# A wait for its own matmuls, behind the first round of each up projection, on TensorE

## The chip, the core and the metric

The kernel runs on one core of one Trainium2 chip. What counts is the time of one execution on the device, in microseconds (us). TensorE (PE in the profile) does the matrix products and loads their weights (PEld), VectorE is DVE, ScalarE is ACT, GpSimd is POOL, and SyncE (SP) issues nearly all of the loads.

## What is computed

Two transformer blocks on 256 tokens of width 2048, in float32. Each block has a mixer (the first two kinds of attention, the second a gated linear recurrence) and behind it a gated feed-forward part of width 5632. The change lies in the feed-forward parts alone:

```
# first block
u = causal_dwconv(h @ w_up[l], conv_w[l], conv_b[l])
gate, up = jnp.split(u, 2, axis=-1)
y = (jax.nn.gelu(gate, approximate=True) * up) @ w_down[l]
x = x + rms_norm(y, post_ffn_norm[l])
...
# second block
up = dwconv3(h @ w_in, w_conv)
gate, val = jnp.split(up, 2, axis=-1)
return (jax.nn.silu(gate) * val) @ w_out
```

`h @ w_up[l]` and `h @ w_in` are the up projections: 256 tokens by 2048 by 11264. The kernel calls them "up1" and "up2", and the projections behind them "down1" and "down2".

## The kernel before

Every product keeps float32 precision by splitting both operands into a high and a low part and summing three products of them: high by high, high by low and low by high. The kernel is one stream of weight chunks. A chunk is 256 rows of a weight matrix by 512 columns (512 KB), and chunks go through a ring of four buffers (`RING`). SyncE loads chunk n into `raw`, ScalarE writes its high part `whi` (L214, `split_hi`), VectorE its low part `wlo` (L219, `split_lo`), and TensorE uses both. Three semaphores count chunks over the whole program: `hi_done`, `lo_done` and `chunk_used`. The last one is raised by the last matmul of a chunk when that matmul has ended, so that its value is the number of chunks that TensorE is through with.

An up projection (`up_pe`) has 11 rounds. A round is 16 chunks (`BODY`): eight for 512 columns of the gate half, gathered in the banks `acc`, and eight for 512 columns of the up half, in the banks `tp`. A chunk is worked by `products_turned`: for each of two slices of 128 rows and each of four tiles of 128 columns, the high weights are loaded and the high and low activations stream past in one matmul of 512 columns (L252), then the low weights are loaded and the high activations stream past in one of 256 columns (L254). One L252 with the L254 behind it is called a pair in this document; a chunk has 8 pairs, a round has 128.

Round 0 is written out (`body(0, True)`), because the turning of the activations (transposes, L306 and L318, and the copies into `ahl` on ScalarE and VectorE, L326 and L337) is woven into its first half, and between its halves stands one small product for the row scale (L574, recorded as two matmuls). Rounds 1 to 10 are a loop of the hardware (`pe.Fori`, L577), whose code stands once. Behind them comes the down projection (`back_pe`, L232 to L234), in three matmuls of 512 columns per step. The order on TensorE is the order of the code; no scheduler moves anything. TensorE's sequencer works through instructions, register steps and waits in this order and hands the matmuls to the engine, ahead of it.

Of the kernel before, what the change touches and what calls it, by code (L numbers as in the profile page):

```python
# [55 lines left out]
def bass_two_blocks(nc, T):  # L56
    with ExitStack() as ctx:
# [5 lines left out]
        def sem(name):  # L63
            if name not in made:
                made[name] = ctx.enter_context(nc.semaphore(name))
            return made[name]
# [120 lines left out]
        hi_done, lo_done, chunk_used = sem("hi_done"), sem("lo_done"), sem("chunk_used")  # L187
# [3 lines left out]
        cb, gb = {}, {}  # L191
# [49 lines left out]
        def products_turned(pe, n, s, half, k0, ready=None, row=None):  # L241

            pe.wait_ge(lo_done, n + 1)
            for k in range(CK):
                kt = k0 + k
                if ready:
                    pe.wait_ge(sem("pre_lo"), lo_ready(ready, kt))
                for ct in range(4):
                    c, o = slice(k * GC + ct * P, k * GC + (ct + 1) * P), part_banks(half, ct // 2)
                    if row and k == 0 and ct == 3:  # L250
                        pe.wait_ge(row, NT + 2)
                    pe.matmul(o[:, ct % 2, :].rearrange("p (a t) -> p a t", a=2), whi[:, s, c], ahl[:, :, kt, :],  # L252
                              start=(kt == 0), stop=False, skip_group_check=True)
                    mm = pe.matmul(o[:, ct % 2, 0:S], wlo[:, s, c], ahi[:, kt, :], start=False, stop=(kt == KT - 1),  # L254
                                   skip_group_check=True)
            mm.then_inc(chunk_used, 1)

        def group(pe, g):

            if not (isinstance(g, int) and g < 2):  # L260
                pe.wait_ge(group_free, g - 1)
# [79 lines left out]
        def lead_pe(pe, ph, c, src, ready):  # L341

            if c == 0:
                pre_pe_by_token(pe, ph, src, ready)
            for q in {2: (2,), 4: (3,)}.get(c, ()):
                pre_pe(pe, ph, q, src, ready)
# [204 lines left out]
        BODY = 2 * CPG  # L551
# [8 lines left out]
        def up_pe(pe, ph, src_ready):  # L560
            def body(i, first):
                for c in range(BODY):
                    if c % CPG == 0 and not first:
                        group(pe, gb[ph] + c // CPG + i * 2)
                    if first:
                        lead_pe(pe, ph, c, x, src_ready)
                    if first and c == 0:
                        pe.wait_ge(group_free, gb[ph])
                    products_turned(pe, cb[ph] + c + i * BODY, c % RING, c // CPG, CK * (c % CPG),
                                    ph if first and c < CPG else None, sem(f"{ph}_row") if first and c == CPG else None)  # L570
                    if first and c == CPG - 1:
                        pe.wait_ge(sem(f"{ph}_row"), NT)
                        pe.wait_ge(sem("ones"), 2)
                        pe.matmul(tp[1][:, 2, :], upones[:, :], cvu[:, 0, :], start=True, stop=True)\  # L574
                          .then_inc(sem(f"{ph}_row"), 1)
            body(0, True)
            with pe.Fori(1, FG) as i:  # L577
                body(i, False)

# [1472 lines left out]
        @block.tensor  # L2052
        def _(pe):
            setup_pe(pe)
            m1_pe(pe)
            up_pe(pe, "up1", x_ready("out1"))
            back_pe(pe, "down1", 1, DCH, sem("up1_hid"))
            m2_pe(pe)
            up_pe(pe, "up2", x_ready("out2"))
            back_pe(pe, "down2", 3, DCH, sem("up2_hid"))  # L2060
# [73 lines left out]
```

## Time and profile before

| what | us |
|---|---|
| median of three timed runs | 2535.77 |
| the three runs | 2527.97, 2535.77, 2537.52 |
| the profiled execution, its own time | 2534.18 |
| its span, first to last instruction | 2532.2 |
| up1: rounds 1 to 10, first matmul of round 1 to first of down1 | 500.35 to 952.62 |
| up2: the same | 1841.21 to 2284.95 |

The trace is of one execution. The three timed ones differ from each other by up to 9.55 us, which is 0.38% of the time. TensorE's busy share is 99% of the span, and its granted clock is 0.999, so that it stands at the higher of its two levels, 2.4 GHz. Ends of matmuls in the profile are modelled; starts are recorded, and a pace is therefore best read from one start to another.

### The profile page before, as it was taken

Reading aid. Unit: us, or ns where it says so; the run is one execution under the profiler, and the core shown is the slowest. Engines: PE = TensorE matmul, PEld = TensorE weight load, DVE = VectorE, ACT = ScalarE, POOL = GpSimd, SP = SyncE. Lnnn points to the kernel's source line nnn. Section 1 sums busy time; section 2 is a strip of 40 time slices with the busy share of each in tenths; the row PEclk is TensorE's granted clock in tenths of the full one; section 3 lists DMA queues with packets and bytes.
Section 4 is the critical chain, followed back from the end, with each engine's and each line's share of the span. In section 5 each row is a group of like instructions: output and inputs, shape, how many; then the busy total and the mean of one; then the engine's idle time right before and its main releaser. Section 6 shows DMA issues by size and latency. Waiting matters only on the chain.

```text
span 2532.2 us, 40555 instructions
## 1 busy us (share of the span) xinstructions
PE 2514.1 (99%) x15445; PEld 2159.4 (85%) x15445; DVE 1651.8 (65%) x2018; ACT 1334.9 (53%) x1753; POOL 222.1 (9%) x94
## 2 busy tenths in 40 slices
PE   9999999999999999999999999999999999999998
PEld 9999877888888888888888888888888888888887
DVE  6665574777676775445586868785667677775444
ACT  5454563655556554444545455454665656554443
POOL 1000000022131221000000000000012121121000
PEclk9999999999999999999999999999999999999999
DMA  7765335566666656556655555555566666666554
GB/s 232 252 205 155 113 127 182 169 183 182 190 186 187 183 182 215 192 191 193 191 176 167 175 153 171 162 163 178 173 189 187 190 189 188 185 194 212 192 193 156
DMA packets 241432, 462.26 MB, mean 183 GB/s; under 512 B 14360, under 2 KB 23377, under 8 KB 240673
## 3 DMA queue, kind: packets, MB, share of 16 engines
q1 hardware_dynamic: 239633, 453.44, 58.0%
q0 software_dynamic: 1568, 7.10, 0.9%
q8 instruction: 86, 1.41, 0.2%
q14 instruction: 33, 0.27, 0.0%
q10 hardware_dynamic: 112, 0.03, 0.0%
HBM read 458.40 MB, written 2.12 MB: 182 GB/s over the span
## 4 chain that ended last, share of the span: by engine, by line
PE 99%; DVE 0%; ACT 0%; issue 0%; POOL 0%; DVEq 0%; POOLq 0%; ACTq 0%
PE acc L232 13%; PE acc L252 13%; PE tp L252 13%; PE acc L234 13%; PE acc L233 13%; PE tp L254 7%; PE acc L254 7%; PE acc L918 3%; PE acc L920 2%; PE acc L921 2%; PE acc L1145 1%; PE acc L1147 1%; PE acc L1146 1%; PE tp L1627 1%; PE acc L926 1%; PE acc L928 1%
## 5 line engine op out<-in xcount | busy, mean ns | idle before, releaser
L219 DVE TENSOR_TENSOR wlo<-raw,whi 128x1024 fp32r<-128x1024 f32 x856 | 1070.7, 1258 | 748.1 <-ACT whi L214 746.5
L214 ACT ACTIVATE whi<-raw 128x1024 fp32r<-128x1024 f32 x856 | 903.1, 1059 | 1005.1 <-PE acc L234 456.2
L252 PE MATMUL acc<-ahl,whi 128*128 128x512 f32 x1408 | 494.2, 395 | 0.6 <-DVE ahl L337 0.6
L252 PE MATMUL tp<-ahl,whi 128*128 128x512 f32 x1408 | 494.2, 395 | 0.0
L254 PE MATMUL tp<-ahl,wlo 128*128 128x256 f32 x1408 | 394.8, 280 | 0.0
L254 PE MATMUL acc<-ahl,wlo 128*128 128x256 f32 x1408 | 394.6, 280 | 0.0
L252 PEld LDWEIGHTS acc<-ahl,whi 128*128 128x128 f32 x1408 | 264.0, 187 | 62.6 <-issue 1.0
L252 PEld LDWEIGHTS tp<-ahl,whi 128*128 128x128 f32 x1408 | 263.9, 187 | 61.9
L232 PE MATMUL acc<-whi,ahl 128*128 128x512 f32 x752 | 298.8, 397 | 0.3 <-DVE ahl L337 0.3
L234 PE MATMUL acc<-whi,ahl 128*128 128x512 f32 x752 | 293.4, 390 | 0.0
L233 PE MATMUL acc<-wlo,ahl 128*128 128x512 f32 x752 | 292.8, 389 | 0.0
L254 PEld LDWEIGHTS tp<-ahl,wlo 128*128 128x128 f32 x1408 | 266.0, 189 | 0.1
L254 PEld LDWEIGHTS acc<-ahl,wlo 128*128 128x128 f32 x1408 | 266.0, 189 | 0.0
L233 PE MATMUL acc<-wlo,hhi 128*128 128x512 f32 x672 | 261.4, 389 | 0.0
L234 PE MATMUL acc<-whi,hlo 128*128 128x512 f32 x672 | 261.4, 389 | 0.0
L232 PE MATMUL acc<-whi,hhi 128*128 128x512 f32 x672 | 261.4, 389 | 0.0
L718 POOL TENSOR_TENSOR cvg<-cvg,cvu 128x1024 f32<-128x1024 f32 x22 | 98.1, 4457 | 1499.4 <-DVE cvu L662 1499.4
L234 PEld LDWEIGHTS acc<-whi,ahl 128*128 128x128 f32 x752 | 141.1, 188 | 30.2
L232 PEld LDWEIGHTS acc<-whi,ahl 128*128 128x128 f32 x752 | 141.2, 188 | 29.6 <-issue 0.5
L233 PEld LDWEIGHTS acc<-wlo,ahl 128*128 128x128 f32 x752 | 141.3, 188 | 27.8
L918 PE MATMUL acc<-ahl,whi 128*128 128x256 f32 x512 | 150.5, 294 | 0.0
L233 PEld LDWEIGHTS acc<-wlo,hhi 128*128 128x128 f32 x672 | 126.1, 188 | 26.3
(271 smaller groups left out, 2968.2 us busy)
## 6 DMA issues: line engine op xcount, KB each, us to landing
raw<-in_w_up_dram SPq DMA_DIRECT2D x176, 512.0 KB, 3.8
raw<-in_ffn_w_in_dram SPq DMA_DIRECT2D x176, 512.0 KB, 4.1
raw<-in_hgrn_w_in_dram SPq DMA_DIRECT2D x160, 512.0 KB, 3.7
raw<-in_w_in_dram SPq DMA_DIRECT2D x88, 512.0 KB, 3.8
raw<-in_w_down_dram SPq DMA_DIRECT2D x88, 512.0 KB, 3.7
raw<-in_ffn_w_out_dram SPq DMA_DIRECT2D x88, 512.0 KB, 3.7
raw<-in_w_out_dram SPq DMA_DIRECT2D x32, 512.0 KB, 3.6
raw<-in_hgrn_w_out_dram SPq DMA_DIRECT2D x32, 512.0 KB, 3.9
```

The source lines that it names most:

```text
L214: act.activation(whi[:, s, :], raw[:, s, :], ACT.Copy).then_inc(hi_done, 1)
L219: dve.tensor_tensor(wlo[:, s, :], raw[:, s, :], whi[:, s, :].bitcast(F32), ALU.subtract).then_inc(lo_done, 1)
L232: pe.matmul(out[:, t, :], xh, whi[:, s, c], start=(kt == 0), stop=False)
L233: pe.matmul(out[:, t, :], xh, wlo[:, s, c], start=False, stop=False)
L234: mm = pe.matmul(out[:, t, :], xl, whi[:, s, c], start=False, stop=(kt == nk - 1))
L252: pe.matmul(o[:, ct % 2, :].rearrange("p (a t) -> p a t", a=2), whi[:, s, c], ahl[:, :, kt, :], start=(kt == 0), stop=False, skip_group_ch ...
L254: mm = pe.matmul(o[:, ct % 2, 0:S], wlo[:, s, c], ahi[:, kt, :], start=False, stop=(kt == KT - 1), skip_group_check=True)
L718: pool.tensor_tensor(cvg[:, :, :], cvg[:, :, :], cvu[:, :, :], ALU.mult).then_inc(sem(f"{ph}_pr"), 1)
L918: pe.matmul(o[:, d], whi[:, s, a], ahi[:, kt, :], start=first and ct % 2 == 0, stop=False, skip_group_check=True)
L920: pe.matmul(o[:, d], whi[:, s, a], alo[:, kt, :], start=False, stop=False, skip_group_check=True)
L921: mm = pe.matmul(o[:, d], wlo[:, s, a], ahi[:, kt, :], start=False, stop=last, skip_group_check=True)
L926: pe.matmul(out[:, t, :], xh, whi[:, s, a], start=first, stop=False)
```

## The change

One wait is added in `up_pe`, between the code of round 0 and the loop over rounds 1 to 10. It runs once in up1 and once in up2.

```
             body(0, True)
+            pe.wait_ge(chunk_used, cb[ph] + BODY)
             with pe.Fori(1, FG) as i:
                 body(i, False)
```

`cb[ph]` is the number of chunks before this projection, and `BODY` is 16, so that TensorE waits for the end of the last matmul of round 0. No instruction is moved; from here on, the lines behind it bear a number higher by one.

TensorE's instructions around the end of round 0 of up1, before the change. `tp` is the bank of the up half, `acc` that of the gate half; the rows of L577 and the row of L243 are steps of the sequencer.

```order
L252 MATMUL tp1<-ahl,whi 128x512
L254 MATMUL tp1<-ahl,wlo 128x256
L577 UNCONDITIONAL_BRANCH
L577 ISA
L243 ISA [waits group_free]
L252 MATMUL acc0<-ahl,whi 128x512 [waits lo_done]
L254 MATMUL acc0<-ahl,wlo 128x256
```

The same place with the change:

```order
L252 MATMUL tp1<-ahl,whi 128x512
L254 MATMUL tp1<-ahl,wlo 128x256
L578 UNCONDITIONAL_BRANCH [waits chunk_used]
L578 ISA
L243 ISA [waits group_free]
L252 MATMUL acc0<-ahl,whi 128x512 [waits lo_done]
L254 MATMUL acc0<-ahl,wlo 128x256
```

The wait stands ahead of the loop's entry, so that the entry's register steps and all the loop's matmuls are behind it. In up2 the same rows stand, with the same wait, and nothing else on any engine differs.

## Rows read from the trace of the kernel before

**Rows 1.** The page's head, its busy shares and its clock slices, TensorE alone.

```profile
span 2532.2 us, 40555 instructions
...
PE 2514.1 (99%) x15445; PEld 2159.4 (85%) x15445; DVE 1651.8 (65%) x2018; ACT 1334.9 (53%) x1753; POOL 222.1 (9%) x94
...
PEclk9999999999999999999999999999999999999999
```

**Rows 2.** The page's chain that ended last, by engine.

```profile
PE 99%; DVE 0%; ACT 0%; issue 0%; POOL 0%; DVEq 0%; POOLq 0%; ACTq 0%
```

**Rows 3.** Waits of TensorE: waiter, waited for, us in total, times, longest.

```profile
PE acc L1145 <- DVE ahl L1460: 2.8, 1, 2.8
...
PE acc L252 <- DVE ahl L337: 0.6, 2, 0.3
```

**Rows 4.** Windows, matmuls of L252 alone: each stretch, its us, then busy (count).

```profile
core 0: us, PE busy (x) PEld busy (x), PEclk, DMA share, GB/s
453.50:458.35 4.85, 4.85 (x15) 2.62 (x15) 1.00 0.35 100
459.93:464.78 4.85, 4.85 (x15) 2.62 (x15) 1.00 0.72 209
466.36:476.95 10.59, 10.59 (x31) 5.62 (x31) 1.00 0.45 143
478.09:500.35 22.26, 22.26 (x65) 11.84 (x64) 1.00 0.71 217
500.35:952.62 452.27, 452.27 (x1281) 240.40 (x1280) 1.00 0.62 185
1794.99:1799.84 4.85, 4.85 (x15) 2.62 (x15) 1.00 0.35 102
1801.42:1806.27 4.85, 4.85 (x15) 2.62 (x15) 1.00 0.72 208
1807.84:1818.23 10.39, 10.39 (x31) 5.62 (x31) 1.00 0.46 147
1819.37:1841.21 21.84, 21.84 (x64) 11.78 (x64) 1.00 0.70 213
1841.21:2284.95 443.74, 443.74 (x1281) 239.25 (x1280) 1.00 0.63 189
```

**Rows 5.** Timeline of TensorE around the start of round 1 in up1: start, us.

```profile
500.23 0.28 PE L254 MATMUL tp<-ahl,wlo 128*128 128x256 f32 x1
500.35 0.40 PE L252 MATMUL acc<-ahl,whi 128*128 128x512 f32 x1
```

**Rows 6.** The line L337, VectorE: ns of one, first and last start.

```profile
L337 DVE SCALAR_TENSOR_TENSOR ahl<-tp,gains,ahl x4: 476/479/484, 452.4 to 453.6; 128x256 fp32r<-128x256 f32 x4
```

**Rows 7.** Timeline where TensorE restarts behind that line, up1's first matmuls.

```profile
452.45 1.66 DVE L337 SCALAR_TENSOR_TENSOR ahl<-tp,gains,ahl 128x256 fp32r<-128x256 f32 x4 [0.36 <-ACT ahl L326]
453.05 0.19 PEld L252 LDWEIGHTS acc<-ahl,whi 128*128 128x128 f32 x1 [0.49 <-issue]
453.08 0.47 PE L252 MATMUL acc<-ahl,whi 128*128 128x512 f32 x1 [0.28 <-DVE ahl L337]
...
453.38 0.28 PE L254 MATMUL acc<-ahl,wlo 128*128 128x256 f32 x1
...
453.73 0.28 PE L254 MATMUL acc<-ahl,wlo 128*128 128x256 f32 x1
```

**Rows 8.** Lines L577 and L243 on TensorE's sequencer: ns min/median/max, first and last start.

```profile
L577 PEldq FUSED_REGOPS  x20: 50/50/50, 497.3 to 2237.8; - x20
...
L577 PEldq COMPARE_BRANCH  x20: 76/208/236, 542.5 to 2281.9; - x20
L577 PEldq MOVE  x2: 33/34/34, 497.2 to 1838.1; - x2
...
L243 PEldq FUSED_REGOPS  x20: 37/37/42, 497.4 to 2237.9; - x20
```

**Rows 9.** Waits of all engines in rounds 1 to 10 of up1.

```profile
DVE wlo L219 <- ACT whi L214: 134.9, 110, 2.1
ACT whi L214 <- PE acc L254: 112.9, 70, 1.8
```

More of the change, by code:

```diff
@@ L576, in up_pe @@
             body(0, True)
+            pe.wait_ge(chunk_used, cb[ph] + BODY)
             with pe.Fori(1, FG) as i:
```

## The prediction

> **What bounds the kernel now.** I read the page first: TensorE is busy for 99% of the span at a granted clock of nine tenths or more in every slice [rows 1], and the chain that ended last is TensorE for 99% [rows 2]. Its waits are few: the longest is 2.8 us, and in the up projections there is one wait for `ahl` at the start of each, 0.6 us for the two [rows 3]. So in the up projections the time is the number of matmuls by the distance from one start to the next, and nothing else. Here the windows show what decides this case [rows 4]. Rounds 1 to 10 have 1280 pairs in either projection, the same code at the same granted clock, 1.00. In up1 they take 452.27 us, which is 353.3 ns a pair, and in up2 443.74 us, 346.7 ns a pair. At 2.4 GHz these are 848 and 832 cycles, 16 apart. The DMA share is 0.62 and 0.63, so the load traffic doesn't tell them apart. I call them the slow and the quick pace; the slow one costs 8.53 us over the ten rounds. VectorE and ScalarE follow at either: they wait for one another and for TensorE [rows 9], and TensorE for none of them.
>
> **Where a pace is taken and where it is kept.** Up to its loop each projection has four places at which a new run of pairs starts: once behind a wait with the engine empty (453.08), twice right behind transposes, once behind the product of the row scale. From the windows between [rows 4], by start-to-start steps: up1 has 4.85/14 = 346 ns, 4.85/14 = 346 ns, then 10.59/30 = 353 ns, 22.26/63 = 353 ns, and the loop at 353.3. Up2 has 346, 346, 10.39/30 = 346, 21.84/63 = 347, and the loop at 346.7. So the slow pace came in at one start, the third of up1 (behind transposes that followed on matmuls without a wait), outlived the row product, and was then held for all of 1280 pairs; in up2 it never came. The pace is a state of the stream, taken when the stream starts and kept while it isn't broken. Both starts behind a real wait, in up1 and in up2, were quick; they run for only 14 steps, which is enough to see the pace. The loop's entry in before is no break: its register steps start at 497.2 to 497.4 [rows 8], while the matmul behind them starts at 500.35 [rows 5], so the sequencer is some 3 us ahead and the stream goes through.
>
> **The wait itself.** What it costs is worked out for up1. The last matmul of round 0 starts at 500.23 and lasts 0.28, so it ends at 500.51, while the next one started at 500.35 [rows 5]: 0.16 us of overlap is lost. From the end of what is waited for to the first matmul I take TensorE's restart at 453.08: `ahl` ended at 452.45 + 0.48 = 452.93 [rows 6, 7], so 0.15 us. The loop's entry steps, hidden before, now stand behind the wait: MOVE, FUSED_REGOPS of L577 and that of L243, from 497.2 to some 497.44 [rows 8], about 0.25 us. The first L254 comes 0.30 us behind its L252 in a restart (453.08 to 453.38), where the usual distance in the quick pace is 0.35 less 0.12, that is 0.23 [rows 5, 7]: 0.08 us. Sum 0.64 us, twice 1.28 us. The wait's lower bound is without the entry steps, 0.39 us. Its upper bound adds the dearest branch, 0.24 us [rows 8], for code that must be fetched: 0.88 us. So 0.8 to 1.8 us for both; I take 1.3, since the entry steps follow the wait in the program.
>
> Nothing else pays. Queued behind the wait on TensorE are only the loop's own matmuls; for them wait ScalarE's next `whi` (L214) and with it VectorE and the loads, which have had to wait for TensorE anyway, 112.9 us of it at `acc` alone in up1 [rows 9]. For those 0.6 us they go on filling the ring. SP's and POOL's queues aren't moved. The clock has no reason to fall: the break is about as long as the wait at the projection's start (0.3 us), where the window behind it shows 1.00 [rows 3, 4].
>
> **A rule set against the rows.** The rows have a pair at 346.7 or 353.3 ns [rows 4]. The Trainium skill, page "TensorE: Matmul & The Clock Gate", section "Back-to-back issue gap", gives start to start as the columns over 2.4 GHz plus 2.5 ns for an isolated matmul, which would be an estimated 325 ns a pair, whatever happened before. It knows no second pace; neither row agrees with it. The same page, section "Step-by-step: what each phase is for", says that the drain of one matmul overlaps the fill of the next, and that this is what makes a stream quick. That speaks against the change: by it, breaking the stream can only lose, and the first rival below would be the outcome.
>
> **The forecast.** The wait empties the engine, so each loop's pace is taken anew at a start of the kind that was quick both times. Up1's loop then goes from 452.27 to 443.74 us, up2's stays at 443.74. From the profiled execution's own time: 2534.18 - 8.53 + 1.28 = 2526.9 us. The median before, 2535.77, lies 1.6 above that execution. Of the three timed runs one took 2527.97, and the others 7.8 and 9.55 more: about the 8.53 of one loop. I read this as an execution with both loops quick and two with one slow loop, so that the kernel before draws its pace in every run. With the change the median would come down to where that quick run was. I give 2527.0.
>
> **The rivals.** First, the wait only costs: the pace depends on something that the wait doesn't reset, or one of the two loops still falls into the slow one in the typical run. For it: slow came at one of only eight starts, so two quick starts behind waits are what chance would mostly give as well. Against it: in this trace the pace was seen to change at a start and nowhere else. Time: 2534.18 + 1.28 = 2535.5 us, no change. Second, on the other side: the start behind the wait lands on the slow pace in both loops. Unlike the starts at 453.08, it comes right behind the engine's own last matmul, with a fixed delay of about half a microsecond, and a fixed delay could fix the bad phase as well as the good one. The price is 8.53 us in up2's loop, 1.28 for the waits, nothing gained in up1: 2534.18 + 9.81 = 2544.0 us. It decides if the restart is 16 cycles a pair slower in more than one loop. Against it are again the two quick starts. Third, the sequencer's lead of 3 us is lost and not won back, and then each turn of the loop shows its branch, 0.24 us and some register steps [rows 8]: 18 turns by about 0.4 us is 7 us on top of the forecast, 2534 us. Against it: after the restart at 453.08 the lead must be built too, and by 497.2 it is 3 us. Fourth, the wait does nothing since the matmuls have ended when it is reached; the sequencer's lead rules that out [rows 5, 8].
>
> **How the numbers follow.** Both loops quick in the typical run: 0.54, at 2525.5 to 2529 (bounds of the wait, and the quick timed run at 2527.97). One loop slow or the wait only costing: 0.30, at 2534 to 2538. Both slow: 0.09, at 2542 to 2546. Lead lost: 0.03. Something unseen, such as a third pace, in either direction: 0.04. The range 2524.5 to 2538.5 takes in the first two and the fourth, 0.87 of the chance; it can't be narrower, as the two likeliest cases lie one loop apart. What a measurement can tell from no change is 0.5%, here 12.7 us, more than one loop's pace is worth. All four cases lie within it (2527.0 is 0.35% below the median, 2544.0 is 0.32% above), so: faster by over 0.5% 0.04, within 0.5% 0.93, slower by over 0.5% 0.03.
>
> **What the profile after would show.** A restart gap in front of the first L252 of round 1 in both projections, 0.5 to 0.9 us from the L252 before it would have come. Rounds 1 to 10: 443.7 us each if I am right; one or both at 452.3 for the rivals. Entry steps of L578 right ahead of that matmul rather than 3 us ahead. In turns of the loop no distance between pairs above 0.36 us; if they show 0.6, the lead is lost. I am wrong in the mechanism if a pace changes in mid-loop, or if both loops are slow behind waits in every run.

## The result, and the profile after

The kernel before has a median of 2532.15 us over 22 runs, the changed one 2537.08 us over 22; the ratio is 1.0029, with a 95% interval of 1.0016 to 1.0043. The change makes the kernel slower, by about 0.3% (the two medians differ by 0.19%, the two means by 0.25%): less than the 0.5% that the prediction took as its bound, but not in the direction that it forecast.

The times don't scatter around a middle. They fall into three groups some 9 us apart, with nothing between them. The median of before even lies in a gap: it is the mean of 2528.53 and 2535.77, and no run took anything near it.

| | up to 2531 | 2533 to 2539 | over 2542 | slow loops |
|---|---|---|---|---|
| before, 22 runs | 11 | 8 | 3 | 14 of 44 |
| changed, 22 runs | 3 | 9 | 10 | 29 of 44 |
| before, all 160 runs of this study | 73 | 74 | 13 | 100 of 320 |

8.53 us is what rounds 1 to 10 of one up projection cost more at the slow pace than at the quick one ([rows 4] of before). So I read a group as the number of loops that ran slow: none, one, two. The last column counts them so. The profiled executions bear it out: those of 2534.18 us (before) and 2535.38 us (changed) have one slow loop, one of 2543.6 us (below) has two, and one of 2527.76 us has none. Over all 160 runs the groups of before have the means 2526.9, 2535.7 and 2545.0 us. They are a little more than 8.53 us apart; in the trace of before the slow pace held from the third start of round 0 on, which is 93 steps more, 0.6 us. The change moved the share of slow loops from 14 of 44 to 29 of 44 (were each loop drawn by itself with one chance, a difference of this size would come up about once in 400 such comparisons), and that, not the wait's own time, is most of the loss.

The profiled execution of the changed kernel took 2535.38 us (span 2533.3). Its chain is TensorE, as in [rows 2], and the clock is the same:

```profile
span 2533.3 us, 40555 instructions
...
PE 2514.7 (99%) x15445; PEld 2159.5 (85%) x15445; DVE 1651.9 (65%) x2018; ACT 1335.0 (53%) x1753; POOL 222.2 (9%) x94
...
PEclk9999999999999999999999999999999999999999
```

The windows of L252 in the changed kernel, to be held against [rows 4]; each row has the stretch, its us, and busy (count). The first two stretches are 14 steps from pair to pair at the very start of up1 and of up2, the third and the last but one are 30 steps ahead of the row product, the fourth and the last are the loops:

```profile
453.31:458.16 4.85, 4.85 (x15) 2.61 (x15) 1.00 0.34 103
1786.93:1791.88 4.95, 4.95 (x15) 2.64 (x15) 1.00 0.35 105
...
466.17:476.77 10.60, 10.60 (x31) 5.63 (x31) 1.00 0.46 144
500.66:944.51 443.85, 443.84 (x1280) 239.36 (x1280) 1.00 0.63 188
1799.88:1810.27 10.39, 10.39 (x31) 5.62 (x31) 1.00 0.46 144
1833.76:2286.12 452.36, 452.36 (x1280) 240.51 (x1280) 1.00 0.62 185
```

Up1 came to the wait in the slow pace (10.60/30 = 353 ns) and left it in the quick one (443.85 us for the loop); up2 came quick (10.39/30 = 346 ns) and left slow (452.36 us). In this execution the wait exchanged the two loops of before and cost its own time. The second row matters as well: behind the wait for `ahl` at the start of up2, with the engine empty, the pace is 4.95/14 = 354 ns, the slow one. In the trace of before both starts of this kind were quick. Over the eleven traces in which this start is unchanged (before, the changed kernel, and nine of the kernels below), 9 of 22 such starts were slow.

The wait itself, TensorE's timeline in up1 (start, us), against [rows 5]:

```profile
499.70 0.28 PE L254 MATMUL tp<-ahl,wlo 128*128 128x256 f32 x1
499.81 0.40 PE L252 MATMUL tp<-ahl,whi 128*128 128x512 f32 x1
500.04 0.28 PE L254 MATMUL tp<-ahl,wlo 128*128 128x256 f32 x1
500.67 0.49 PE L252 MATMUL acc<-ahl,whi 128*128 128x512 f32 x1 [0.34 <-DVE wlo L219]
501.00 0.28 PE L254 MATMUL acc<-ahl,wlo 128*128 128x256 f32 x1
501.12 0.40 PE L252 MATMUL acc<-ahl,whi 128*128 128x512 f32 x1
```

The step from L252 to L252 across the wait is 0.86 us where 0.35 is usual, the next is 0.45, together 0.61 us more. The releaser that is named is `wlo`; the wait that the edit puts there is the one for TensorE's own matmul, and I read the gap as that one. The steps of the loop's entry now stand right ahead of the matmul at 500.67, where in [rows 8] they were 3 us ahead of it:

```profile
L578 PEldq FUSED_REGOPS  x20: 50/50/50, 500.5 to 2238.1; - x20
...
L578 PEldq MOVE  x2: 29/32/34, 500.4 to 1833.5; - x2
```

### The profile page after: what moved, and what is told of

It reads as the page before. It is cut to its first block, busy times and chain, and to the rows that moved or that the text cites. A ratio compares the mean times of both kernels' runs of the same rounds, so it can differ in the third digit from the quotient of the medians.

```text
span 2533.3 us, 40555 instructions
## 1 busy us (share of the span) xinstructions
PE 2514.7 (99%) x15445; PEld 2159.5 (85%) x15445; DVE 1651.9 (65%) x2018; ACT 1335.0 (53%) x1753; POOL 222.2 (9%) x94
## 4 chain that ended last, share of the span: by engine, by line
PE 98%; ACT 1%; DVE 0%; issue 0%; POOL 0%; DVEq 0%; ACTq 0%; POOLq 0%
PE acc L232 13%; PE acc L252 13%; PE acc L234 13%; PE acc L233 13%; PE tp L252 13%; PE acc L254 7%; PE tp L254 6%; PE acc L919 3%; PE acc L922 2%; PE acc L921 2%; PE acc L1146 1%; PE acc L1148 1%; PE acc L1147 1%; PE tp L1628 1%; PE acc L927 1%; PE acc L929 1%
## 5 line engine op out<-in xcount | busy, mean ns | idle before, releaser
L219 DVE TENSOR_TENSOR wlo<-raw,whi 128x1024 fp32r<-128x1024 f32 x856 | 1070.6, 1258 | 749.4 <-ACT whi L214 747.7
L252 PE MATMUL acc<-ahl,whi 128*128 128x512 f32 x1408 | 494.5, 395 | 1.3 <-DVE wlo L219 0.7
L252 PE MATMUL tp<-ahl,whi 128*128 128x512 f32 x1408 | 494.2, 395 | 0.0
L252 PEld LDWEIGHTS acc<-ahl,whi 128*128 128x128 f32 x1408 | 264.0, 187 | 63.9 <-DVE wlo L219 1.3
L252 PEld LDWEIGHTS tp<-ahl,whi 128*128 128x128 f32 x1408 | 263.9, 187 | 61.9
```

The lines of the kernel that those rows point to most:

```text
L219: dve.tensor_tensor(wlo[:, s, :], raw[:, s, :], whi[:, s, :].bitcast(F32), ALU.subtract).then_inc(lo_done, 1)
```

## The experiments

What had to be told apart: does the wait turn the pace into the other one ("turn"), does each restart draw it by chance ("draw"), does it belong to the stage ("place"), or is it set by where the restart falls in time, to a fraction of a matmul ("phase")? All diffs are against the kernel before unless another is named. Each kernel is compared with runs of before on the same chip; a ratio is to those runs, with its 95% interval in brackets; "groups" gives a kernel's runs with no, one and two slow loops, read from their times, where these fall so.

### The wait in each round

```
             def body(i, first):
+                if not first:
+                    pe.wait_ge(chunk_used, cb[ph] + i * BODY)
                 for c in range(BODY):
```

> The wait for its own matmuls stands at the head of every round of the loop, ten times in each up projection instead of once. In the trace after, the wait turned up1 from the slow pace (353.3 ns a pair) to the quick one (346.7) and up2 from quick to slow. Theory 'turn': a restart behind an emptied engine turns whichever pace was there into the other. Then the rounds alternate, slow, quick, slow, quick, 128 pairs each (45.2 and 44.4 us), in every execution alike, and the time is that of an execution before with two quick loops (about 2527) plus 20 waits of 0.60 us plus ten slow rounds of 0.85 us: 2547.5 us with little spread. Theory 'draw': each restart draws its pace anew, slow in about two of three: no alternation, some 13 of 20 rounds slow, about 2550 us and differing by a few us from run to run. Theory 'place': the pace hangs on the stage and not on the wait: all ten rounds of a projection alike.

Measured: median 2545.06 us (2544.06 to 2546.95, 6 runs), ratio 1.0053 [1.0034, 1.0072]. Windows of L252 over rounds 0 to 6 of up1, from the second pair of a round to its last, 126 steps (the first row is the 62 steps of round 0 behind the row product, 353 ns each, the second all of round 0 with its breaks):

```profile
481.36:503.27 21.91, 21.91 (x63) 11.64 (x63) 1.00 0.66 212
...
456.78:503.27 46.49, 44.80 (x127) 23.65 (x127) 1.00 0.55 175
504.48:548.16 43.68, 43.68 (x128) 23.56 (x127) 1.00 0.58 182
549.35:593.87 44.52, 44.52 (x128) 23.68 (x127) 1.00 0.58 185
595.06:638.74 43.68, 43.68 (x128) 23.62 (x127) 1.00 0.58 182
639.93:684.45 44.52, 44.52 (x127) 23.68 (x127) 1.00 0.58 184
685.65:729.33 43.68, 43.68 (x127) 23.62 (x127) 1.00 0.59 183
730.52:775.04 44.52, 44.52 (x127) 23.67 (x127) 1.00 0.57 184
```

43.68/126 is 346.7 ns, 44.52/126 is 353.3: the rounds alternate strictly, at all 20 transitions of this execution, in up1 and in up2. The spread of the times, 2.9 us, fits a kernel with a fixed number of slow rounds. So in this kernel the outcome of a restart isn't drawn, and it doesn't belong to the stage. Each wait here costs less than the changed kernel's, as it stands behind the loop's entry: 0.74 to 0.76 us across instead of 0.86. The time follows: 2526.9 + 20 x 0.49 + 10 x 0.85 = 2545.2 us. "Turn" seemed right, and was put to the next tests.

### A wait in up1 alone

```
# against the changed kernel
-            pe.wait_ge(chunk_used, cb[ph] + BODY)
+            if ph == "up1":
+                pe.wait_ge(chunk_used, cb[ph] + BODY)
```

> The changed kernel with the wait in up1 alone, up2 as before. 'Turn': in each execution up1's loop has the pace that its round 0 did not have, so up1 is slow in the share of runs in which before it was quick (about 2 in 3), up2 in about 1 in 3; median about 2536. 'Draw' gives the same shares, but within the trace the pace of the loop need not be the opposite of that of round 0. 'Place' (the wait only costs): median of before plus 0.6 us.

Measured: median 2535.55 us (2528.19 to 2544.7), ratio 1.0017 [0.9996, 1.0038], groups 3, 5, 2: 9 of 20 loops slow, between the shares of before and of the changed kernel, as two loops of which one has the wait should be. But in its trace up1 was slow ahead of the wait (353.4 ns) and slow behind it (353.3 ns). The wait at this place doesn't always turn the pace.

### The same restart with one more satisfied wait

```
# against the kernel with the wait in each round
                     pe.wait_ge(chunk_used, cb[ph] + i * BODY)
+                    pe.wait_ge(hi_done, 1)
```

> As the kernel that waits for its own matmuls at the head of each round, which gave strict turns of slow and quick rounds, but with one more wait behind it that is long satisfied (hi_done at 1 or more), so that each restart comes some 0.05 us later. 'Turn' (an emptied engine turns the pace, whatever the delay): the rounds still alternate, 2545 us plus 20 times 0.05, 2546 us. 'Phase' (the restart keeps a fixed distance from the last matmul, and the pace taken depends on where that distance lets the stream come in): with another distance the pattern is another one, such as all rounds quick (2537 us), all slow (2554 us) or a turn of another length, and it is regular, the same in up1 and up2 after a few rounds. 'Draw': no pattern.

Measured: median 2547.39 us (2540.45 to 2549.91, 5 runs), ratio 1.005 [1.0016, 1.0085]. The alternation is gone. In the trace the rounds 0 to 10 read, with Q for quick and S for slow, Q Q S S Q S Q S S S S in up1 and Q Q Q Q Q Q Q S S Q S in up2. Two slow rounds in a row in up1 (2 and 3) and two quick ones in a row in up2 (1 and 2):

```profile
548.52:593.03 44.51, 44.51 (x127) 23.71 (x127) 1.00 0.62 185
594.24:638.76 44.52, 44.52 (x127) 23.73 (x127) 1.00 0.61 182
1846.81:1890.48 43.67, 43.67 (x127) 23.59 (x127) 1.00 0.62 183
1891.68:1935.36 43.68, 43.68 (x128) 23.61 (x127) 1.00 0.62 183
```

The steps across the waits are, but for one of 0.79, the same 0.74 to 0.76 us as without the second wait, so it didn't delay the restart by anything that can be seen there, and yet the outcomes changed. That ends "turn" as a rule. It is also more than the plain form of "phase" said: the pattern isn't regular, and up2 kept the quick pace over six restarts and then lost it. The step behind the restart, from its first L252 to the second, does show something, if the starts in the trace are read to the nanosecond. Over the restarts right behind such a wait in all traces of this study it was 450 ns eight times, six of them here in up2, with the quick pace behind it each time, and 452 ns or more thirteen times, four of them here, with the slow pace behind it each time. Between 444 and 448 ns both came up.

### Small products in place of the wait

```
                         group(pe, gb[ph] + c // CPG + i * 2)
+                    if c == 0 and not first:
+                        keep_busy(pe, acc[0][:, 0, 0:P], 1 if ph == "up1" else 8)
```

> No wait is added. At the head of each of the rounds 1 to 10 TensorE does small products whose result is overwritten (128 columns each): one in up1, eight in up2. They break the stream of pairs without emptying the engine. 'Turn', if it holds for emptied engines alone: the pace stays through the loop, as it stayed over the row product of round 0. 'Draw': if any break draws, the rounds of a loop differ, without a pattern. If a break shifts the stream by a fixed amount, one and eight products give two different but regular patterns. Time: ten times about 0.2 us in up1 and ten times about 0.95 us in up2, so some 11 us over before, plus what the pace does (8.5 us a slow loop).

> No wait; one product of 128 columns whose result is overwritten at the head of each of the rounds 1 to 10, in both up projections. With one product in up1 the pace went quick, slow, slow, quick, slow, then quick for the last six rounds, and with eight in up2 it stayed quick after one slow round. 'Phase': such a break is a fixed map of the stream's state and the quick state is one that it leads back to itself; so both projections are quick from some round on in every run, whatever they began with, and the groups of times 8.5 us apart are gone: 2526 us (both loops quick before) plus 20 breaks of 0.11 us plus 2 to 4 slow rounds of 0.85 us: 2530 us. 'Draw' with a small chance of slow at such a break: slow rounds anywhere, one in five, 2531.5 us, with the late rounds no quicker than the early ones.

The second of these kernels has one product in both projections (`1` instead of the choice). Measured: 2537.62 us (2536.77 to 2540.92), ratio 1.0023 [1.0007, 1.004], and 2532.92 us (2529.16 to 2535.83), ratio 1.0008 [0.9993, 1.0024]. These breaks add no wait (with one product, the step across is 0.43 us where 0.35 is usual), and they change the pace too. With one product, up1 went through rounds 0 to 10 as Q S S Q S Q Q Q Q Q Q, in both kernels, on different occasions, exactly alike; up2 of the second went S and then Q ten times, and up2 of the first, with eight products, Q Q S and then Q eight times. From there on each break led the quick pace back to itself. That the sequence is repeated is against "draw". But the median of the second lies 3 us above what two to four slow rounds give (2530), and its runs spread by 6.7 us, so in other runs the stream probably reached the quick pace later than in the trace.

### Six such breaks, and then the loop

```
+                    if c % CPG == 0 and not first and isinstance(i, int):
+                        keep_busy(pe, (tp if c else acc)[0][:, 0, 0:P], 1)
...
             body(0, True)
-            with pe.Fori(1, FG) as i:
+            for i in (1, 2, 3):
+                body(i, False)
+            with pe.Fori(4, FG) as i:
```

> The rounds 1 to 3 are written out, with one overwritten product of 128 columns at the head of each half of each round (six breaks a projection); rounds 4 to 10 are the loop, without breaks. 'Phase': six breaks lead to the quick state nearly always, and the loop keeps it: 2526 us plus 12 breaks of 0.11 us plus one or two slow half rounds: 2528 to 2529 us in nearly all runs. 'Draw': one slow loop in five, so times in two or three groups, up to 8 us above that. If code that is written out costs TensorE fetches of instructions, gaps show in rounds 1 to 3.

A miss: median 2540.12 us (2534.0 to 2545.14), ratio 1.0033 [1.0016, 1.0051]. With the breaks 64 pairs apart instead of 128 they didn't lead to the quick pace: in the trace up1 left the last break slow and stayed slow for seven and a half rounds, while up2 was quick. No gaps from written-out code appear. So it isn't the number of such breaks alone that brings the quick pace.

### The single wait at other distances

```
             body(0, True)
+            pe.wait_ge(chunk_used, cb[ph] + BODY)
+            body(1, False)
-            with pe.Fori(1, FG) as i:
+            with pe.Fori(2, FG) as i:
```

The second kernel adds one overwritten product of 128 columns between the wait and round 1; the third a second wait behind round 1, with round 2 written out as well:

```
# the second, against the first, in body
+                    if c == 0 and isinstance(i, int) and i == 1:
+                        keep_busy(pe, acc[0][:, 0, 0:P], 1)
# the third, against the first
             body(1, False)
+            pe.wait_ge(chunk_used, cb[ph] + 2 * BODY)
+            body(2, False)
-            with pe.Fori(2, FG) as i:
+            with pe.Fori(3, FG) as i:
```

> The changed kernel's single wait, at the same place, but round 1 is written out behind it instead of standing in the loop, so that the steps of the loop's entry (0.25 us) no longer lie between the wait and the first matmul; the loop runs rounds 2 to 10. The restart comes at another fixed distance (some 0.37 us from the last matmul's start to the next one less than 0.62 us). 'Phase' (the pace taken hangs on where the restart falls, to a fraction of a matmul): the share of slow loops moves away from the 29 of 44 of the changed kernel, to either side, and may come near none or all; times 2526 or 2543 us in most runs. 'Turn' (an emptied engine turns the pace): the share stays at two in three, median 2536. 'Draw': the same as turn.

> As the kernel with the wait and round 1 written out, with one overwritten product of 128 columns between the wait and round 1's first matmul. 'Phase': a third distance gives a third share of slow loops. If the product of 128 columns alone decides (in the kernels with one at each round the pace was quick in 16 of 20 and 15 of 20 rounds), the slow share is 1 in 4: median 2527 to 2530. 'Turn': two in three, 2536.

> Two waits in each up projection, behind round 0 and behind round 1, both rounds 1 and 2 written out. 'Turn': turned twice, so that each loop has the pace it has in the kernel before: slow in 1 of 3, median 2527 plus four waits of 0.4 us, plus one turned round, 2530. 'Phase' with a fixed outcome for this distance: if the kernel with one wait so placed gives nearly only one pace, this one gives it too, or the opposite of it, in all runs; if its map is mixed, groups 8.5 us apart.

Measured: 2544.53 us (2542.58 to 2546.87), ratio 1.0056 [1.0038, 1.0073]; 2544.86 us (2542.9 to 2546.99), ratio 1.0047 [1.003, 1.0063]; 2546.55 us (2544.49 to 2547.6), ratio 1.0058 [1.004, 1.0076]. Groups 0, 0, 10 in all three: 60 loops of 60 slow. The trace of the first, windows of L252 in round 0 behind the row product (60 steps) and of round 1 of up1 (126 steps), and the same of up2 with all the rest of its rounds:

```profile
479.87:500.67 20.80, 20.80 (x61) 11.22 (x61) 1.00 0.71 215
502.05:546.56 44.51, 44.51 (x127) 23.67 (x127) 1.00 0.62 183
1820.24:1841.04 20.80, 20.80 (x62) 11.22 (x61) 1.00 0.67 208
1842.42:2293.96 451.54, 451.54 (x1279) 240.13 (x1279) 1.00 0.63 185
```

Quick ahead of the wait (346.7), slow behind it (353.3). Its restart:

```profile
501.02 0.39 PE L252 MATMUL tp<-ahl,whi 128*128 128x512 f32 x1
501.25 0.28 PE L254 MATMUL tp<-ahl,wlo 128*128 128x256 f32 x1
501.59 0.50 PE L252 MATMUL acc<-ahl,whi 128*128 128x512 f32 x1
501.93 0.28 PE L254 MATMUL acc<-ahl,wlo 128*128 128x256 f32 x1
```

0.57 us across the wait instead of 0.86, and 0.46 for the next step, so that the wait costs 0.34 us instead of 0.61 (the difference, 0.27, is what the loop's entry adds behind a wait), and yet every loop is slow. In the kernel with two waits the second one met a slow stream and left it slow. Here the wait neither turns nor draws: in this form it always gives the slow pace. The same wait with a loop's entry behind it gave 29 slow loops of 44. That the outcome hangs on the place in time at which the restart falls fits these four kernels, but isn't shown by them: they differ in the code behind the wait as well, and with the product the distance is another one (0.65 us across, 0.43 for the next step) and the outcome the same. (The expectation of that kernel counts 16 and 15 quick rounds of 20 in the two kernels with small products; the traces have 16 and 17.)

### Another order of the matmuls

The four column tiles of a slice in the order of two high and two low matmuls, and of four and four, in place of high and low in turn:

```
-                for ct in range(4):
+                for cp in range(2):
+                  for ct in (2 * cp, 2 * cp + 1):
                     pe.matmul(o[:, ct % 2, :].rearrange("p (a t) -> p a t", a=2), whi[:, s, c], ahl[:, :, kt, :],
                     ...
+                  for ct in (2 * cp, 2 * cp + 1):
                     mm = pe.matmul(o[:, ct % 2, 0:S], wlo[:, s, c], ahi[:, kt, :], start=False, stop=(kt == KT - 1),
```

and for the second kernel one loop `for ct in range(4)` around the high ones, and one around the low ones.

> The order of the matmuls in a slice of an up projection is changed: two matmuls of 512 columns (high weights of two column tiles) and then the two of 256 columns, instead of 512 and 256 in turn. Same matmuls, same sums, no added wait. If the slow pace belongs to the strict turn of 512 and 256 columns, it is gone and every execution has 346.7 ns a pair or less: about 2527 us in all runs, 0.2% under the median of before. If the two paces belong to any stream of loads and matmuls of this size, the times still fall into groups some 8.5 us apart. If two short matmuls in a row expose the loading of weights, a pair takes longer: each 10 ns of it are 28 us.

> The order within a slice of an up projection is four matmuls of 512 columns and then four of 256. The order of two and two had one pace in all runs, 348.2 ns a pair, and lost 1.5 ns to the quick pace. If the loss lies at the changes between 512 and 256 columns, it is halved with half as many changes: 347.4 ns, 2528 us in all runs. If the slow pace needs the turn of 512 and 256 alone, no group of slower runs appears. If the four short matmuls in a row expose the weight loads, a pair costs more: over 350 ns, 2536 us or more.

The order of two and two: 2530.53 us, and 2529.82 to 2532.01 in all ten runs, ratio 0.9997 [0.9979, 1.0014]. There are no groups, and in its trace both projections run at the same pace, 348.2 ns. In its timeline the first high matmul of each group of four comes every 0.695 us on average:

```profile
700.38 0.62 PE L253 MATMUL acc<-ahl,whi 128*128 128x512 f32 x2
700.84 0.40 PE L257 MATMUL acc<-ahl,wlo 128*128 128x256 f32 x2
701.08 0.63 PE L253 MATMUL acc<-ahl,whi 128*128 128x512 f32 x2
701.54 0.39 PE L257 MATMUL acc<-ahl,wlo 128*128 128x256 f32 x2
701.77 0.63 PE L253 MATMUL acc<-ahl,whi 128*128 128x512 f32 x2
```

So the two paces were seen only in the strict turn of 512 and 256 columns. The order of four and four: 2538.02 us (2534.26 to 2539.79), ratio 1.0016 [0.9999, 1.0033], 350.8 ns a pair in its trace. Fewer changes between the lengths didn't halve the loss, and the time is that of the expectation's last case; whether its reason, exposed weight loads, is the right one wasn't followed.

### Products with zeros

In the second half of round 0 a product with zeros (256 columns) is added to the sums at the head of a chunk, which leaves them as they are. GpSimd writes the zeros once, early in the program (not shown below), and TensorE waits for them ahead of its first pair in each projection.

```
                     if first and c == 0:
                         pe.wait_ge(group_free, gb[ph])
+                        pe.wait_ge(sem("zt"), 1)
+                    if first and c > CPG:
+                        pe.wait_ge(lo_done, cb[ph] + c + 1)
+                        pe.matmul(part_banks(1, 0)[:, 0, 0:S].rearrange("p (a t) -> p a t", a=4),
+                                  whi[:, c % RING, 0:P], bcast(zt[:, :], 1, 4), start=False, stop=False,
+                                  skip_group_check=True)
```

With three products the condition is `CPG < c < CPG + 4`, with one it is `c == CPG + 1`.

> No wait. In the second half of round 0, at the head of seven of its chunks, a product with zeros (256 columns) is added to the sums, which leaves them as they are; each costs some 0.12 us, 1.7 us in all. 'Phase': seven fixed shifts of the same kind, eight pairs apart, lead to one state, as the breaks at round heads did, and the loop keeps it: one group of times, 2528 us if the state is quick, 2545 if it is slow. 'Draw': slow in 1 of 5 to 1 of 3, groups 8.5 us apart.

> Three products with zeros instead of seven. In the trace with seven the stream was in turn in the two quick patterns from the first of them on, but it entered quick. If three shifts bring a slow stream to the quick state too: one group of times at 2527.2 us (1.0 us less than with seven), and about 0.2% below the mean of before, which is what its slow loops cost. If three don't do: a second group 8.5 us above, in fewer than one loop in three.

> One product with zeros in each projection. A single shift can turn a quick stream slow as well as the other way. If one does: 2526.7 us in all runs. If it maps only some of the slow stream's states to quick: groups 8.5 us apart, with fewer slow loops than before (1 in 3). If the first shift is no better than none: as before.

Measured, with seven, three and one product: 2528.15 us (2527.69 to 2530.63), ratio 0.9985 [0.9968, 1.0002]; 2527.47 us (2526.15 to 2529.23, 12 runs), ratio 0.9982 [0.9967, 0.9998]; 2526.81 us (2525.74 to 2528.72), ratio 0.9979 [0.9962, 0.9995]. No slow loop in 64. The last two are faster than before beyond their intervals. In the traces with seven and with one product the stream was quick when it reached them, in both projections, so that they might not be what did it. In the trace with three, up1 came slow. Its windows are 30 steps ahead of the row product, 6 steps behind it, 7 steps behind the first product with zeros, and everything behind the third:

```profile
466.87:477.47 10.60, 10.60 (x31) 5.63 (x31) 1.00 0.40 133
478.60:480.72 2.12, 2.12 (x7) 1.13 (x7) 1.00 0.87 317
481.20:483.64 2.44, 2.44 (x8) 1.32 (x8) 1.00 0.85 252
486.99:944.25 457.26, 457.26 (x1320) 247.32 (x1320) 1.00 0.59 189
```

That is 353 ns, 353, then some 348, and 346.7 for the rest: here the stream came to the first product slow and left it quick. How much of the gain is due to the products is asked of a control, the kernel with one product without that product:

```
# against the kernel with one product
-                    if first and c == CPG + 1:
+                    if first and c < 0:
```

> The kernel with one product with zeros, without that product, but with the zeros written and the wait for them at the start of each projection. If the product makes the loops quick: the groups of before are back, 2526, 2535 and 2544 us, one loop in three slow. If something else of that kernel does it: one group at 2526.7 us again.

Measured: 2526.88 us (2525.46 to 2535.05), ratio 0.9969 [0.9951, 0.9988], groups 9, 1, 0: one slow loop in 20, where before has 19 in 50 on the same chip and 100 in 320 in all. So most of the gain doesn't need the products. What is left of the edit is the wait for the zeros at the start of each projection, which is satisfied when it is reached (they are written at 18.9 us), and GpSimd's writing of them; the two weren't told apart, and how they act isn't shown. Behind the transposes of round 0 the traces have the slow pace in 1 of 14 projections with this wait and in 6 of 22 without it; at the very first start it is as frequent with it (8 of 14) as without (9 of 22). The expectation that the groups would come back was wrong. To see what the products do, a stream was sent to them that should be slow, behind a wait of the kind that gave 60 slow loops of 60:

```
# against the kernel with one product
+                    if first and c == CPG + 1:
+                        pe.wait_ge(chunk_used, cb[ph] + CPG + 1)
-                    if first and c == CPG + 1:
+                    if first and c == CPG + 4:
```

and, for three products behind the forced wait, `CPG + 4 <= c < CPG + 7`.

> A wait for TensorE's own matmuls at the head of chunk 9 of round 0, then one product with zeros at the head of chunk 12. Behind the wait the slow pace is expected (all loops of ten runs were slow behind a wait of that kind). If one such product turns the slow stream quick: the trace shows 353 ns between chunks 9 and 12 and 346.7 from there on, and all runs lie at 2527.5 us (two waits of 0.35 and two products of 0.12 over 2526). If it leaves it slow: 2544 us in all runs. If it depends on a finer state: groups.

> The same with products with zeros at the heads of chunks 12, 13 and 14. If such shifts lead any state to the quick one in one to three steps: quick from the last of them on in either projection, 2528 us in all runs, also where one product alone wasn't enough. If slow maps to slow under this shift: 2545 us, and the quick runs of the kernels with these products have another cause.

With three: 2527.93 us (2527.27 to 2529.34), ratio 0.998 [0.9959, 1.0], groups 10, 0, 0. The windows of its up2 show the three steps: behind the forced wait (21 steps), between the first two products (6 steps), between the second and the third (6 steps), and the loop:

```profile
1815.94:1823.36 7.42, 7.42 (x23) 3.95 (x22) 1.00 0.75 253
1824.18:1826.29 2.11, 2.11 (x8) 1.13 (x7) 1.00 0.68 224
1827.13:1829.20 2.07, 2.07 (x7) 1.12 (x7) 1.00 0.74 231
1835.21:2278.60 443.39, 443.39 (x1280) 239.37 (x1280) 1.00 0.59 189
```

7.42/21 is 353 ns, slow; 2.11/6 is 352, still slow; 2.07/6 is 345, quick (at six steps the hundredths blur the exact value); and the loop runs quick. In its up1 the first product did. With one product only: 2528.07 us (2526.84 to 2544.35), ratio 0.9977 [0.9958, 0.9996], groups 7, 2, 1. The profiled execution was the slowest of the ten, and in it both loops stayed slow:

```profile
482.78:490.54 7.76, 7.76 (x23) 4.12 (x23) 1.00 0.78 252
502.32:953.00 450.68, 450.68 (x1277) 239.63 (x1276) 1.00 0.58 185
1843.20:2295.10 451.90, 451.90 (x1280) 240.30 (x1280) 1.00 0.58 185
```

With three such products behind the forced wait 20 loops of 20 were quick, with one 16 of 20. That the stream was slow ahead of them is seen in the two traces, in all four projections, and is taken over from there for the other runs.

### The changed kernel's wait behind a known state

Seven products with zeros as above, and then the changed kernel's wait:

```
# against the kernel with seven products
             body(0, True)
+            pe.wait_ge(chunk_used, cb[ph] + BODY)
             with pe.Fori(1, FG) as i:
```

> The kernel with seven products with zeros in round 0 (all loops quick, 2528 us) and behind round 0 the changed kernel's wait. If the outcome of the wait is fixed by the state of the stream ahead of it and the distance of the restart, this kernel has one outcome, the state ahead being one and the same: either all loops slow (2528 + 1.2 + 17.1 = 2546 us; in the trace after, a quick stream became slow) or all quick (2529 us), in every run. If the wait itself draws, the times fall into three groups as with the changed kernel, 2529, 2538 and 2546, two loops in three slow.

Measured: 2546.95 us (2538.04 to 2548.65), ratio 1.0046 [1.0026, 1.0065], groups 0, 3, 7: 17 slow loops of 20. Without the wait this kernel had 0 of 20 (on another chip), so that it is the wait that makes loops slow. From a quick stream the changed kernel's wait gives the slow pace nearly always, but not always; the expectation of one and the same outcome held in 17 of 20. Its steps across the wait are 0.845 and 0.850 us in the trace, against 0.857 and 0.855 in the changed kernel.

## Why the prediction was wrong

**What bounds the kernel** held: the chain, the clock and the 1280 pairs at one of two paces explain both traces and the groups of all runs. That the kernel before draws its pace in each run, read from three times and one trace, held as well: 160 runs fall into the groups.

**Where a pace is taken and kept** held in its first half. A pace changes at a break and never in mid-loop, in any of these traces. What was made of the second half failed: "Both starts behind a real wait, in up1 and in up2, were quick". Two cases of two were taken for a property of waits. The next trace had a start of the same kind that was slow (the row 1786.93:1791.88 above), and with 9 of 22 such starts slow, two quick ones in a row come up about one time in three.

**The wait itself** was sized well: 0.64 us each was forecast, 0.61 measured, with the entry's steps behind the wait as worked out: without them 0.39 was forecast, and the kernel with round 1 written out shows 0.34. The granted clock of both loops stayed at 1.00.

**The rule set against the rows.** By the Trainium skill, page "TensorE: Matmul & The Clock Gate", section "Step-by-step: what each phase is for", breaking the stream can only lose the overlap of drain and fill. The trace agrees as far as the wait goes: the two cost 1.2 us together, the entry's steps included. The larger part of the loss, the pace, isn't in the rule.

**The forecast** failed with the step "each loop's pace is taken anew at a start of the kind that was quick both times". In its place: 29 slow loops of 44. By the means, 14 slow loops to 29 over 22 runs is 0.68 of a loop a run, 5.8 us, and the waits are 1.2; the means of the runs, 2533.31 and 2539.61, differ by 6.3 us, so that the two terms explain the loss within the noise. The second rival, both loops slow, was given 0.09 and took place in 10 runs of 22; its reason, that "a fixed delay could fix the bad phase as well as the good one", fits the wait with round 1 written out, slow in 20 loops of 20, though that it is the delay wasn't shown. The first rival, one loop slow, took 9 of 22. The case that was forecast came in 3 of 22. The third and the fourth rival didn't occur: the turns of the loop show no exposed branches, and the wait does wait.

**The chances.** That the effect lies within 0.5% held, since one loop's pace is worth 0.34% and the shift of the median is a part of it. The direction was decided by a guess on how a restart falls, and deserved even chances. Nothing in a single trace could tell the two apart, but the same rows show the asymmetry: before had the slow pace in few loops, so a change that draws anew has more to lose than to win.

**What stays open.** What the phase is measured against, and why the changed kernel's wait gives both outcomes (17 of 20 from a quick stream, and both from a slow one) while the one with round 1 written out gives one. A second, satisfied wait, which left the step across the restart as it was, changed a strict pattern; the step behind the restart tells the outcome in some cases and not in others. Other engines tell the paces apart too: VectorE's line L219 takes 1.29 us on average in the slow loop of before and 1.32 in the quick one, and the changed kernel, with the loops exchanged, has the same two values the other way round. Whether that is an effect of the pace or a part of what sets it, no run asked. It wasn't settled either why the kernel with nothing but the zeros and the satisfied wait for them has the quick pace so much more often.

## What to carry to other kernels

A stream of matmuls of two lengths in turn can have more than one steady pace, and here a wait or a small product moved it from one to the other for hundreds of microseconds. When the times of an unchanged kernel fall into groups, count them and find the stretch whose pace makes the difference before judging an edit: an edit of half a microsecond may be seen through a shift of 8.5. And a property read from two starts is a guess; a form that has one outcome takes the question away instead of leaving the answer to luck. Here that is the order of two and two, at 2530.5 us no quicker than before on the median, or the three products with zeros, no slow loop in 44.

## What wasn't expected of the hardware

TensorE runs this pair of matmuls, 512 and 256 columns with a weight load each, at 346.7 or 353.3 ns, at the same granted clock of 1.00 and with nearly the same DMA share (0.63 and 0.62), and holds either through all 1280 pairs of a loop. Which one it held was set by a wait for its own matmuls without exception in one form (60 slow loops of 60 in three kernels), in alternation in another (20 turns of 20), and in a mixture in a third. The best kernels of the study, with one and with three products with zeros and without any but with their wait, took 2526.81, 2527.47 and 2526.88 us against 2534.32 and 2534.2 of before on the same chips; their gain is the slow loops that didn't occur: the runs of before without a slow loop have a mean of 2526.9 us.
